# A streaming-encoder step on one core: the edges of the expert stage, and the walk of one eviction

## Chip, core and metric

The kernel runs on one core of a Trainium2 chip. The metric is the device time of one launch in microseconds; lower is better. Several runs of the same kernel give a median, and one more execution is taken with the hardware profiler. Engines are named as in the profile: PE is the tensor engine, DVE the vector engine, ACT the scalar engine, POOL the GpSimd engine and SP the sync engine, which here only issues DMAs.

## What is computed

One layer of a transformer-like encoder for 640 tokens (512 of a prompt, 8 x 16 of samples), D = 1024. The change lies in its last part, a retrieval over 128 x 128 = 16384 single-neuron experts:

```python
s1 = q1 @ sub_keys_1.T ; s2 = q2 @ sub_keys_2.T       # 8 heads, 128 keys each
idx, top_s = top-16 of (top-16 of s1) + (top-16 of s2)  # per token and head
gate = softmax(top_s)
f = sum over the 128 chosen experts of  gelu(x . u[idx]) * gate * v[idx]
y = x + gt2 * rmsnorm(f, g_ffn_post)
```

`u` and `v` are tables of 16384 x 1024 floats, 64 MB each.

## The kernel before

The kernel is a row of phases with a barrier of all engines between them. The last two are the gates stage (`phase_gates`) and the expert stage (`phase_experts`).

The 640 tokens are treated in two ways. The first 256 (`GT` = 2 tiles of 128) are *gathered*: POOL issues 512 indirect DMAs (`rows`), each fetching one expert's row of `u` or `v` for 128 tokens, and DVE works on each row (a dot product, or `vacc += egate * row`). The other 384 (`DN`) are *dense*: every expert is computed for them on PE, and a table of gates, mostly zeros, decides what counts.

**The gates stage** writes that table, `gates[block, key, key, token]`, for 6 blocks of 64 tokens. A *group* is 4 tokens, so there are 96 groups. For each, DVE marks one-hot rows of the keys (`first`, `second`, L1858 to L1863), ACT multiplies three of the four by their gates (`weigh`, L1899), PE multiplies them into a 128 x 128 square per token (L1879), and ACT copies the four squares from PSUM into a staging buffer `stage[e]`, [128, 128 keys, 64 tokens] (the *eviction*, L1906). In ACT's program the weighing of group n+1 stands ahead of the eviction of group n. `stage` has two buffers of 32 KB per partition; SP stores each full one as one DMA of 4 MB (L1843). SP also loads the first four tiles of `u` here.

**The expert stage** goes through 128 chunks (`q`) of 128 experts. For each chunk PE transposes the `u` tile (two halves, L2096), ACT and DVE split it into a high and a low part (`uT_h`, `uT_l`), PE multiplies with the dense tokens ("hidden", 24 matmuls, L2107), ACT takes Gelu (`gl`, L2067), POOL multiplies by the gates of this chunk (`gt`, L2035, the *weighing by gates*), ACT and DVE split that (`a_h`, `a_l`), and PE multiplies it with the split `v` tile ("outputs", 18 matmuls, L2119). PE runs hidden of chunk q, then outputs of chunk q-1. Each engine's order is written out by hand: POOL issues the gathers that are due before each weighing by gates; DVE works on four gathered rows per chunk; SP loads `u`, `vraw` (two buffers) and, for every four chunks, `gt` (two buffers) out of the stored table.

At the end (`finish`, five tiles of 128 tokens, in order) ACT squares the tile with a sum (L2079) and takes the root (L2082), DVE scales and adds `x` (L2183, L2187), and SP stores the tile (L2006).

The places that the change touches: `vraw` of the expert stage lay in the memory of `stage[0]`, as did `v`, `a`, `gl`; `gt` and five of the 12 `rows` buffers lay in `stage[1]`. So SP issued the first `gt` load, and behind it `vraw`, after all table stores had landed (L1981 to L1987).

Of the kernel before, what the change touches and what calls it, by code (L numbers as in the profile page):

```python
# [26 lines left out]
ALU = mybir.AluOpType  # L27
# [1762 lines left out]
TB = 64  # L1790


def phase_gates(nc, A, env):
# [11 lines left out]
    env["env"].update(h=h, u=u)  # L1805
# [29 lines left out]
    with nc.Block() as block:  # L1835
        @block.sync
        def _(sp):
            for i in range(len(u)):
                sp.dma_start(u[i][:], A["u_experts"][0, i * P:(i + 1) * P, :]).then_inc(u_in, 16)
            with sp.Fori(0, BLOCKS // 2) as pair:  # L1840
                for e in range(2):
                    sp.wait_ge(S["table_ready"], pair * (2 * PB) + (e + 1) * PB + G)
                    sp.dma_start(A["gates"][pair * 2 + e], stage[e][:]).then_inc(stored[e], 16)  # L1843
            sp.wait_ge(u_in, 16 * len(u))

        @block.gpsimd
# [38 lines left out]
        def _(act):  # L1885
# [16 lines left out]
            def body(n, g, e, at, token, last):  # L1902
# [3 lines left out]
                act.activation(stage[e][:, :, bass.ds(at, G)].rearrange("p i n -> p n i"), PS[:, g, :].rearrange("p (n i) -> p n i", n=G),  # L1906
# [6 lines left out]
def phase_experts(nc, A, env):  # L1913
# [3 lines left out]
    eidx, egate, htok = (env[k] for k in ("eidx", "egate", "htok"))  # L1917
# [9 lines left out]
    v = [[sb(f"v_{'hl'[s]}{i}", 146 + 8 * i + 4 * s, [P, D], F32R) for s in (HI, LO)] for i in range(2)]  # L1927
    a = [[sb(f"a_{'hl'[s]}{i}", 162 + 3 * i + 1.5 * s, [P, DN], F32R) for s in (HI, LO)] for i in range(2)]
    gl = [sb(f"gl{i}", 168 + 1.5 * i, [P, DN]) for i in range(2)]
    gt = [sb(f"gt{i}", 171 + 6 * i, [P, BLK, QUAD, TB]) for i in range(2)]  # L1930
    EARLY = (10, 62, 66, 70, 74, 78, 203)
# [4 lines left out]
    junk = sb("ej", 114, [P, D])  # L1936
# [4 lines left out]
    v_in, g_in = ([sem(f"ex_{n}_in{i}") for i in range(2)] for n in "vg")  # L1941
    row_in = [sem(f"ex_row_in{i}") for i in range(R)]
    y_out = [sem(f"ex_y_out{i}") for i in range(2)]
    y_dram = [A["y_p"][0, t * P:(t + 1) * P, :] for t in range(PT)] + [A["y_s"].rearrange("b q d -> (b q) d")]

    SLOTS = GT * H * TOPK
    LAG = 2 * TOPK
    steps = [("u", k) for k in range(LAG)]
    for k in range(SLOTS):
        steps.append(("v", k))  # L1950
        if k + LAG < SLOTS:
            steps.append(("u", k + LAG))
# [17 lines left out]
    with nc.Block() as block:  # L1970
        @block.sync
        def _(sp):
            def body(i, first, last):
                for q in range(QUAD):
# [9 lines left out]
                    if not (first and q < 2):  # L1984

                        sp.wait_ge(S["v_lo"], i * QUAD + q - 1)
                    sp.dma_start(vraw[q % 2][:], A["v_experts"][0, bass.ds(i * (QUAD * P) + q * P, P), :]).then_inc(v_in[q % 2], 16)  # L1987

            def gates(i, e, first):

                if not first:

                    sp.wait_ge(S["weighed"], i * QUAD)
# [10 lines left out]
            for t in range(NT):  # L2004
                sp.wait_ge(S["y_ready"], t + 1)
                sp.dma_start(y_dram[t], y[t % 2][:]).then_inc(y_out[t % 2], 16)  # L2006
            sp.wait_ge(y_out[0], 16 * 3)
            sp.wait_ge(y_out[1], 16 * 2)

        @block.gpsimd  # L2010
        def _(pool):
            def gather(n):
                kind, k = steps[n]
# [7 lines left out]
                t, j = divmod(k, H * TOPK)  # L2021
                pool.indirect_dma_start(out=rows[n % R][:], out_offset=None, in_=A["u_experts" if kind == "u" else "v_experts"][0],  # L2022
                                        in_offset=bass.IndirectOffsetOnAxis(ap=eidx[:, t, j:j + 1], axis=0)).then_inc(row_in[n % R], 16)

            for n in range(R - PER):
                gather(n)
            for q in range(NCH):
                for n in range(PER * q + R - PER, min(PER * (q + 1) + R - PER, len(steps))):
                    gather(n)
# [8 lines left out]
        def _(act):  # L2038
# [11 lines left out]

            turned(0, 0)
            turned(0, 1)
            for q in range(NCH):
                if q + 1 < NCH:
# [17 lines left out]
            for t in range(NT):  # L2072
                if t < GT:
                    act.wait_ge(S["summed"], (t + 1) * H * TOPK)
                else:
                    act.wait_ge(S["f_psum"], NCH)
                if t:
                    act.wait_ge(S["f_sq"], t)
                act.activation(junk[:].rearrange("p (b n) -> p b n", b=2), result(t), ACT.Square, accum_out=stat[:, 0, t:t + 1]  # L2079
                               ).then_inc(S["f_sq"], 1)  # L2080
# [159 lines left out]
```

## Time and profile before

| | |
|---|---|
| median of 3 runs (range) | 2402.19 us (2400.85 to 2405.74) |
| profiled execution, its own time | 2401.34 us |
| its span | 2399.6 us |
| PE busy | 2093.4 us, 87% of the span |
| DVE busy | 1635.9 us, 68% |
| ACT busy | 839.6 us, 35% |
| POOL busy | 876.6 us, 37% |
| gates stage | about 995 to 1170 us of the span |
| expert stage | about 1171 us to the end |

Busy time is summed over the whole span, and each stage has its own limit, so the prediction reads the two stages apart. Times of rows are microseconds from the start of the span.

### The profile page before, as it was taken

The page shows a single profiled execution, that of the slowest core. Times are in us where ns is not written, and L with a number is a line of the kernel's source. Part 1 is how long each engine was busy: PE and PEld are TensorE (multiplying, and loading weights), DVE is VectorE, ACT ScalarE, POOL GpSimd, SP SyncE. Part 2 cuts the span into 40 slices and gives each one's busy share as a digit, 9 for nine tenths or more (in the row PEclk, how much of TensorE's full clock was granted, in tenths as well). Part 3 has the DMA queues.
Part 4 walks back from the last instruction along what each step waited for, and adds up shares of the span by engine and source line. Part 5 has one row for each costly group of instructions (what it writes and reads, how often), then busy time and mean ns, then how long its engine had stood idle before and what let it go on. Part 6 is the DMA issues. An engine that isn't in the chain of part 4 may idle for free.

```text
span 2399.6 us, 34976 instructions
## 1 busy us (share of the span) xinstructions
PE 2093.4 (87%) x12419; PEld 1826.7 (76%) x12419; DVE 1635.9 (68%) x3217; ACT 839.6 (35%) x1532; POOL 876.6 (37%) x708
## 2 busy tenths in 40 slices
PE   6997888688897993266499999999999999999997
PEld 6894676466755993155489989899889899999986
DVE  2413355334333899988478888888888888888888
ACT  2303344222321111299533333333333333333333
POOL 0001111000000000100167667767667667777762
PEclk9998999899998996599899999999999999999999
DMA  7311232333221000033699999999999999999994
GB/s 247 107 36 52 88 106 89 119 101 130 104 106 73 1 2 1 35 140 140 262 330 366 366 350 373 361 356 368 347 368 363 357 370 356 367 369 354 368 358 176
DMA packets 193494, 537.67 MB, mean 224 GB/s; under 512 B 19797, under 2 KB 76410, under 8 KB 191610
## 3 DMA queue, kind: packets, MB, share of 16 engines
q1 hardware_dynamic: 119376, 267.53, 31.4%
q0 software_dynamic: 73728, 268.47, 29.3%
q8 instruction: 44, 0.72, 0.1%
q10 hardware_dynamic: 298, 0.55, 0.1%
q14 instruction: 48, 0.39, 0.0%
HBM read 505.35 MB, written 31.15 MB: 224 GB/s over the span
## 4 chain that ended last, share of the span: by engine, by line
PE 47%; DMA 4%; issue 3%; DVE 2%; ACT 2%; SPq 0%; ACTq 0%; DVEq 0%; POOLq 0%; POOL 0%
PE PS L2107 20%; PE PS L2119 19%; PE PS L2096 4%; DMA u<-in_u_experts 3%; PE PS L1879 3%; ACT first L1899 1%; DMA vraw<-in_v_experts 1%; DMA gates<-stage 1%; DVE vacc L2170 0%; DVE first L1862 0%; DVE v_l L2197 0%; DVE rows L2156 0%; DVE yo L2183 0%; DVE yo L2187 0%; ACT stage L1906 0%
## 5 line engine op out<-in xcount | busy, mean ns | idle before, releaser
L2022 POOL DMA_INDIRECT rows<-in_u_experts,eidx x256 | 424.4, 1658 | 247.7 <-POOLq L160 166.9
L2107 PE MATMUL PS<-h_hi,uT_h 128*128 128x384 f32 x1024 | 355.4, 347 | 0.0
L2107 PE MATMUL PS<-h_hi,uT_l 128*128 128x384 f32 x1024 | 345.0, 337 | 0.0
L2107 PE MATMUL PS<-h_lo,uT_h 128*128 128x384 f32 x1024 | 344.0, 336 | 0.0
L2170 DVE SCALAR_TENSOR_TENSOR vacc<-rows,egate,vacc 128x1024 f32<-128x1024 f32 x254 | 329.6, 1298 | 2.2
L2146 DVE TENSOR_TENSOR uT_l<-PS,uT_h 128x512 fp32r<-128x512 f32 x256 | 177.2, 692 | 202.7 <-ACT uT_h L2042 202.7
L2156 DVE SCALAR_TENSOR_TENSOR rows<-rows,htok 128x1024 f32<-128x1024 f32 x256 | 310.1, 1216 | 6.6 <-DMA rows<-in_u_experts,eidx 6.5
L2119 PE MATMUL PS<-v_h,a_h 128*128 128x512 f32 x768 | 310.9, 405 | 0.0
L2119 PE MATMUL PS<-v_l,a_h 128*128 128x512 f32 x768 | 300.0, 391 | 0.0
L2022 POOL DMA_INDIRECT rows<-in_v_experts,eidx x256 | 271.4, 1060 | 58.9 <-issue 43.0
L2042 ACT ACTIVATE uT_h<-PS 128x512 fp32r<-128x512 f32 x256 | 153.1, 598 | 367.4 <-PE PS L2096 367.4
L2119 PE MATMUL PS<-v_h,a_l 128*128 128x512 f32 x768 | 238.1, 391 | 0.0
L2035 POOL TENSOR_TENSOR gl<-gl,gt 128x384 f32<-128x384 f32 x128 | 133.9, 1046 | 236.0 <-ACT gl L2067 236.0
L2107 PEld LDWEIGHTS PS<-h_lo,uT_h 128*128 128x128 f32 x1024 | 194.0, 189 | 0.0
L2107 PEld LDWEIGHTS PS<-h_hi,uT_h 128*128 128x128 f32 x1024 | 193.9, 189 | 0.0
L2107 PEld LDWEIGHTS PS<-h_hi,uT_l 128*128 128x128 f32 x1024 | 193.3, 189 | 0.0
L2096 PE MATMUL PS<-const,u 128*128 128x128 f32 x1024 | 155.9, 275 | 33.0 <-DVE uT_l L2146 25.1
L2067 ACT ACTIVATE gl<-PS 128x384 f32<-128x384 f32 x128 | 62.9, 491 | 335.0 <-PE PS L2107 335.0
L2096 PEld LDWEIGHTS PS<-const,u 128*128 128x128 f32 x1024 | 126.8, 141 | 59.0 <-DVE uT_l L2146 26.0
L2119 PEld LDWEIGHTS PS<-v_h,a_l 128*128 128x128 f32 x768 | 144.3, 188 | 31.3
L1879 PE MATMUL PS<-first,second 128*128 128x128 f32 x768 | 109.7, 287 | 64.8 <-issue 43.4
L2197 DVE TENSOR_TENSOR v_l<-vraw,v_h 128x1024 fp32r<-128x1024 f32 x128 | 156.1, 1220 | 14.7 <-ACT v_h L2062 14.7
(342 smaller groups left out, 3618.1 us busy)
## 6 DMA issues: line engine op xcount, KB each, us to landing
u<-in_u_experts SPq DMA_DIRECT2D x128, 512.0 KB, 8.1
vraw<-in_v_experts SPq DMA_DIRECT2D x128, 512.0 KB, 5.7
gates<-stage SPq DMA_DIRECT2D x6, 4096.0 KB, 11.5
gt<-gates SPq DMA_DIRECT2D x32, 768.0 KB, 9.6
wada_b<-in_w_ada SPq DMA_DIRECT2D x16, 1024.0 KB, 5.1
wada<-in_w_ada SPq DMA_DIRECT2D x8, 1024.0 KB, 11.9
kc<-in_cache_sb_k SPq DMA_DIRECT2D x8, 1024.0 KB, 7.3
vc<-in_cache_sb_v SPq DMA_DIRECT2D x8, 1024.0 KB, 5.4
```

The costliest lines, as they stand in the source:

```text
L1879: mm = pe.matmul(PS[:, g, j * NKEYS:(j + 1) * NKEYS], second[g][:, j, :], first[g][:, j, :], start=True, stop=True)
L2022: pool.indirect_dma_start(out=rows[n % R][:], out_offset=None, in_=A["u_experts" if kind == "u" else "v_experts"][0], in_offset=bass.Indir ...
L2035: pool.tensor_tensor(act_by_block, act_by_block, gt[e][:, :, c, :], ALU.mult).then_inc(S["weighed"], 1)
L2042: act.activation(uT[q % 2][HI][:, 4 * b:4 * b + 4, :], PS[:, 0, :].rearrange("p (k n) -> p k n", k=4), ACT.Copy).then_inc(S["uT_hi"], 1)
L2067: act.activation(gl[q % 2][:], PS[:, 1, 0:DN], ACT.Gelu).then_inc(S["gelu"], 1)
L2096: mm = pe.transpose(PS[:, 0, j * P:(j + 1) * P], u[q % UR][:, k * P:(k + 1) * P], ident)
L2107: mm = pe.matmul(PS[:, 1, 0:DN], uT[q % 2][w][:, k, :], h[m][:, k, :], start=k == 0 and (w, m) == PASSES[0], stop=k == KD - 1 and (w, m) = ...
L2119: mm = pe.matmul(PS[:, 2 + 2 * t + b, :], a[q % 2][w][:, t * P:(t + 1) * P], v[q % 2][m][:, b * 512:(b + 1) * 512], start=fresh and (w, m) ...
L2146: dve.tensor_tensor(uT[q % 2][LO][:, 4 * b:4 * b + 4, :], PS[:, 0, :].rearrange("p (k n) -> p k n", k=4), uT[q % 2][HI][:, 4 * b:4 * b + 4 ...
L2156: dve.scalar_tensor_tensor(out=row[:], in0=row[:], scalar=1.0, in1=htok[:, t, :], op0=ALU.mult, op1=ALU.mult, accum_out=dots[:, t, j:j + 1 ...
L2170: dve.scalar_tensor_tensor(out=vacc[:, t, :], in0=row[:], scalar=egate[:, t, j:j + 1], in1=vacc[:, t, :], op0=ALU.mult, op1=ALU.add).then_ ...
L2197: dve.tensor_tensor(v[q % 2][LO][:], vraw[q % 2][:], v[q % 2][HI][:], ALU.subtract).then_inc(S["v_lo"], 1)
```

## The change

1. The eviction of the gates stage reads PSUM and writes `stage` in another order: keys outside, the group's four tokens inside. Before it was tokens outside, keys inside.
2. The memory map of the expert stage is drawn anew. `vraw` and three `rows` buffers lie where `hT` lay, which is free after POOL has split it (`h_split`). SP loads the first two `vraw` tiles, and POOL issues the first three gathers, in the gates stage behind `h_split`. `rows` has 11 buffers instead of 12.
3. The last of the six table stores is issued as four DMAs of 1 MB (32 keys each). The first `gt` load waits for the first of the four; the second `gt` load, and POOL's gather number 5, wait for all four.
4. The first of the five final tiles, whose rows are all summed after chunk 71, is squared in chunk 72 and finished in chunk 73. Results are written into `vacc` or into one buffer per tile, so no store has to land before the next tile.

The diff, cut to its core:

```diff
+PARTS = 4
+LAG = 2 * TOPK
+AHEAD = 3
...
 def phase_gates(nc, A, env):
...
+    vraw = [sb(f"vraw{i}", 46 + 4 * i, [P, D]) for i in range(2)]
+    rows = [sb(f"rows{i}", at, [P, D]) for i, at in enumerate((54, 58, 62, 10, 203, 176, 180, 184, 188, 192, 196))]
...
-            with sp.Fori(0, BLOCKS // 2) as pair:
-                for e in range(2):
-                    sp.wait_ge(S["table_ready"], pair * (2 * PB) + (e + 1) * PB + G)
-                    sp.dma_start(A["gates"][pair * 2 + e], stage[e][:]).then_inc(stored[e], 16)
+            sp.wait_ge(h_split, 2)
+            for i in range(2):
+                sp.dma_start(vraw[i][:], A["v_experts"][0, i * P:(i + 1) * P, :]).then_inc(v_in[i], 16)
+            for b in range(BLOCKS - 1):
+                sp.wait_ge(S["table_ready"], (b + 1) * PB + G)
+                sp.dma_start(A["gates"][b], stage[b % 2][:]).then_inc(stored[b % 2], 16)
+            sp.wait_ge(S["table_ready"], BLOCKS * PB + G)
+            for i in range(PARTS):
+                keys = slice(i * NKEYS // PARTS, (i + 1) * NKEYS // PARTS)
+                sp.dma_start(A["gates"][BLOCKS - 1, :, keys, :], stage[1][:, keys, :]).then_inc(parts[i], 16)
...
+            pool.wait_ge(h_split, 2)
+            for n in range(AHEAD):
+                gather(pool, A, eidx, steps, rows, row_in, n)
...
-                act.activation(stage[e][:, :, bass.ds(at, G)].rearrange("p i n -> p n i"), PS[:, g, :].rearrange("p (n i) -> p n i", n=G),
+                act.activation(stage[e][:, :, bass.ds(at, G)], PS[:, g, :].rearrange("p (n i) -> p i n", n=G),
                                ACT.Copy).then_inc(S["table_ready"], 1)
...
 def phase_experts(nc, A, env):
...
-    uT = [[sb(f"uT_{'hl'[s]}{i}", 46 + 8 * i + 4 * s, [P, KD, P], F32R) for s in (HI, LO)] for i in range(2)]
+    uT = [[sb(f"uT_{'hl'[s]}{i}", 138 + 8 * i + 4 * s, [P, KD, P], F32R) for s in (HI, LO)] for i in range(2)]
-    vraw = [sb(f"vraw{i}", 138 + 4 * i, [P, D]) for i in range(2)]
-    rows = [sb(f"rows{i}", at, [P, D]) for i, at in enumerate(EARLY + (183, 187, 191, 195, 199))]
+    LATE = 5
-    y = [sb(f"yo{i}", 106 + 4 * i, [P, D]) for i in range(2)]
+    y = [vacc[:, t, :] for t in range(GT)] + [sb(f"yo{i}", 106 + 4 * i, [P, D])[:] for i in range(DT)]
+    first_done = steps.index(("v", H * TOPK - 1)) // PER + 1
...
-                        for stored in env["gates_stored"]:
-                            sp.wait_ge(stored, 16 * (BLK // 2 + 1))
+                        sp.wait_ge(env["gates_stored"][0], 16 * (BLK // 2 + 1))
+                        sp.wait_ge(env["gates_stored"][1], 16 * (BLK // 2))
+                        sp.wait_ge(env["gates_parts"][0], 16)
                         sp.dma_start(gt[0][:], A["gates"][0:BLK, :, 0:QUAD, :].rearrange("b p c n -> p b c n")).then_inc(g_in[0], 16)
...
-                if n == len(EARLY):
-                    for stored in env["gates_stored"]:
-                        pool.wait_ge(stored, 16 * (BLK // 2 + 1))
+                if n == LATE:
+                    for part in env["gates_parts"]:
+                        pool.wait_ge(part, 16)
...
+            act.wait_ge(env["gates_stored"][0], 16 * (BLK // 2 + 1))
             turned(0, 0)
             turned(0, 1)
             for q in range(NCH):
+                if q == first_done:
+                    squared(0)
+                if q == first_done + 1:
+                    rooted(0)
...
+                if q == first_done:
+                    variance(0)
+                if q == first_done + 1:
+                    finish(0)
-            for t in range(NT):
+            for t in range(1, NT):
+                variance(t)
                 finish(t)
```

Three places show how the instructions stand. First SP, from the last stores of the gates stage to its first waits on chunks; before the change the stores are in a loop over pairs of blocks.

```order
L1843 DMA gates<-stage_7322 128x8192
L1842 REGISTER_ALU
L1843 ISA
L1843 DMA gates<-stage_7323 128x8192
L1840 REGISTER_ALU
L1840 COMPARE_AND_BRANCH
L1835 UNCONDITIONAL_BRANCH
L1971 UNCONDITIONAL_BRANCH
L1983 DMA gt_8847<-gates 128x6x256
L1987 DMA vraw_8835<-in_v_experts 128x1024
```

The same place on SP after the change.

```order
L1869 DMA u_7337<-in_u_experts 128x1024
L1872 DMA vraw_7338<-in_v_experts 128x1024
L1872 DMA vraw_7339<-in_v_experts 128x1024
L1875 DMA gates<-stage_7322 128x8192
...
L1879 DMA gates<-stage_7323 128x2048 x4
L1865 UNCONDITIONAL_BRANCH
L2001 UNCONDITIONAL_BRANCH
L2014 DMA gt_8845<-gates 128x6x256
L2019 DMA vraw_7338<-in_v_experts 128x1024
```

The loads of the first two `vraw` tiles have moved from behind the first `gt` load to ahead of all stores, and the last store is four.

Second POOL, from its split of `hT` in the gates stage to its first weighing by gates, before the change: behind the branches twelve gathers stand ahead of that weighing (the first and the last are shown).

```order
L1850 TENSOR_TENSOR h_lo<-hT,h_hi 128x3072
L1835 UNCONDITIONAL_BRANCH
L159 ISA
L2010 UNCONDITIONAL_BRANCH
L2022 DMA rows_8849<-in_u_experts,eidx 128x1024
...
L2022 DMA rows_8860<-in_u_experts,eidx 128x1024
L2035 TENSOR_TENSOR gl_8845<-gl_8845,gt_8847 128x384
```

The same place on POOL after the change.

```order
L1886 TENSOR_TENSOR h_lo<-hT,h_hi 128x3072
L1812 DMA rows_7340<-in_u_experts,eidx 128x1024
L1812 DMA rows_7341<-in_u_experts,eidx 128x1024
L1812 DMA rows_7342<-in_u_experts,eidx 128x1024
L1865 UNCONDITIONAL_BRANCH
...
L1812 DMA rows_7344<-in_u_experts,eidx 128x1024
L1812 DMA rows_7345<-in_u_experts,eidx 128x1024
...
L1812 DMA rows_7350<-in_u_experts,eidx 128x1024
L2065 TENSOR_TENSOR gl_8847<-gl_8847,gt_8845 128x384
```

Three gathers now stand in the gates stage; of the eight that are left ahead of the weighing, the third (`rows_7345`) is the one that waits for all four parts, so six are issued behind that wait.

Third ACT, in chunks 72 and 73 after the change (`htok` takes the Square's unused output, `stat` its sums; a chunk's own rows are `uT_h`, `v_h`, `gl`, `a_h` and now and then `dots`).

```order
L2120 ACTIVATE a_h_8851<-gl_8848 128x384
L2088 ACTIVATE htok,stat<-vacc 128x1024
L2072 ACTIVATE uT_h_8838<-PS 128x512
L2079 ACTIVATE dots<-dots 128x16
...
L2120 ACTIVATE a_h_8849<-gl_8847 128x384
L2093 ACT_TABLE_LOAD
L2093 ACTIVATE stat<-stat 128x1
L2072 ACTIVATE uT_h_8836<-PS 128x512
L2111 ACTIVATE v_h_8843<-vraw_7339 128x1024
L2116 ACT_TABLE_LOAD
L2116 ACTIVATE gl_8848<-PS 128x384
```

The Square, the root and the two table loads are new in the loop; before, these chunks held the other rows alone.

## Rows read from the trace of the kernel before

**Rows 1.** Windows view: stretch, length, busy us (count) by engine, clock, DMA share, GB/s.

```profile
1090.00:1117.00 27.00, 17.97 (x129) 15.38 (x129) 22.65 (x50) 27.00 (x65) 0.00 (x0) 1.00 0.36 155
...
1184.00:1200.00 16.00, 0.00 (x0) 0.00 (x0) 2.47 (x4) 0.00 (x0) 4.68 (x5) 0.57 1.03 403
...
2100.00:2200.00 100.00, 99.95 (x545) 90.79 (x544) 84.00 (x111) 33.43 (x55) 71.51 (x55) 1.00 0.99 366
```

**Rows 2.** Chain that ended last, between the stages: start us, us, what.

```profile
1169.80 14.16 DMA gates<-stage
1184.48 16.41 DMA vraw<-in_v_experts
...
1212.70 4.11 PE PS L2119 x18
```

**Rows 3.** Groups of the gates stage, the eviction: count, busy, mean ns, idle before.

```profile
L1906 ACT ACTIVATE stage<-PS 128x512 f32 (+1 forms) x96 | 118.1, 1230 | 0.9 <-PE PS L1879 0.9
```

**Rows 4.** Timeline, gates stage: its start, then two groups in the middle.

```profile
1010.56 0.96 ACT L1899 ACTIVATE first<-first,sel 128x128 f32<-128x128 f32 x3
...
1100.97 1.28 ACT L1906 ACTIVATE stage<-PS 128x512 f32 x1
...
1101.80 1.19 ACT L1899 ACTIVATE first<-first,sel 128x128 f32<-128x128 f32 x3
...
1103.09 1.13 PE L1879 MATMUL PS<-first,second 128*128 128x128 f32 x8 [0.57 <-issue]
...
1104.35 1.28 ACT L1906 ACTIVATE stage<-PS 128x512 f32 x1
```

**Rows 5.** Timeline, ACT in an early chunk of the expert stage.

```profile
1217.28 0.60 ACT L2042 ACTIVATE uT_h<-PS 128x512 fp32r<-128x512 f32 x1 [2.83 <-PE PS L2096]
1217.78 1.05 ACT L2062 ACTIVATE v_h<-vraw 128x1024 fp32r<-128x1024 f32 x1
```

**Rows 6.** Timeline: SP's four loads, the last eviction, PE's restarts.

```profile
995.40 1.75 SPq L1839 DMA_DIRECT2D u<-in_u_experts  x4
...
1168.60 1.02 ACT L1906 ACTIVATE stage<-PS 128x512 f32<-128x512 f32 x1 [0.33 <-PE PS L1879]
...
1171.21 0.63 PE L2096 MATMUL PS<-const,u 128*128 128x128 f32 x4 [2.64 <-PEq L160]
...
1205.03 1.12 PE L2096 MATMUL PS<-const,u 128*128 128x128 f32 x4 [22.26 <-DVE uT_l L2146]
```

**Rows 7.** Timeline, POOL and ACT at the first weighing by gates.

```profile
1185.96 0.94 POOL L2022 DMA_INDIRECT rows<-in_u_experts,eidx  x1 [0.30 <-issue]
...
1203.85 0.99 POOL L2035 TENSOR_TENSOR gl<-gl,gt 128x384 f32<-128x384 f32 x1 [13.23 <-ACT gl L2067]
...
1204.87 0.52 ACT L2071 ACTIVATE a_h<-gl 128x384 fp32r<-128x384 f32 x1 [0.62 <-POOL gl L2035]
```

**Rows 8.** Tile view of `gt`, over all its 32 loads.

```profile
DMA to landing us min/median/max: 7.9/9.6/14.3
```

**Rows 9.** Timeline, ACT and DVE in a chunk in the middle of the expert stage.

```profile
1717.23 0.60 ACT L2042 ACTIVATE uT_h<-PS 128x512 fp32r<-128x512 f32 x1 [2.84 <-PE PS L2096]
...
1717.86 0.69 DVE L2146 TENSOR_TENSOR uT_l<-PS,uT_h 128x512 fp32r<-128x512 f32 x1 [1.01 <-ACT uT_h L2042]
...
1721.43 0.49 ACT L2067 ACTIVATE gl<-PS 128x384 f32<-128x384 f32 x1 [2.55 <-PE PS L2107]
```

**Rows 10.** Timeline, the last tiles' finish.

```profile
2378.97 1.28 ACT L2082 ACT_TABLE_LOAD   x1
...
2383.04 0.61 PE L2119 MATMUL PS<-v_h,a_l 128*128 128x512 f32 x2
...
2383.77 1.28 DVE L2183 SCALAR_TENSOR_TENSOR yo<-vacc,stat,gffn 128x1024 f32<-128x1024 f32 x1
2384.61 0.20 ACT L2079 ACTIVATION_READ_ACCUMULATOR ej<-PS 128x1 f32 x1
2385.09 1.22 DVE L2187 TENSOR_TENSOR yo<-yo,x 128x1024 f32<-128x1024 f32 x1
2386.24 0.14 DVE L2176 TENSOR_SCALAR stat<-stat 128x1 f32<-128x1 f32 x1
```

More of the change, by code:

```diff
@@ L1790, with gather_order, gather @@
 TB = 64
+PARTS = 4
+SLOTS = GT * H * TOPK
+LAG = 2 * TOPK
+AHEAD = 3
+def gather_order():
+    steps = [("u", k) for k in range(LAG)]
+    for k in range(SLOTS):
+        steps.append(("v", k))
+        if k + LAG < SLOTS:
+            steps.append(("u", k + LAG))
+    return steps
+def gather(pool, A, eidx, steps, rows, row_in, n):
+    kind, k = steps[n]
+    t, j = divmod(k, H * TOPK)
+    slot = n % len(rows)
+    pool.indirect_dma_start(out=rows[slot][:], out_offset=None, in_=A["u_experts" if kind == "u" else "v_experts"][0],
+                            in_offset=bass.IndirectOffsetOnAxis(ap=eidx[:, t, j:j + 1], axis=0)).then_inc(row_in[slot], 16)
 def phase_gates(nc, A, env):
@@ L1804, in phase_gates @@
     u = [sb(f"u{i}", 106 + 4 * i, [P, D]) for i in range(4)]
-    env["env"].update(h=h, u=u)
+    vraw = [sb(f"vraw{i}", 46 + 4 * i, [P, D]) for i in range(2)]
+    rows = [sb(f"rows{i}", at, [P, D]) for i, at in enumerate((54, 58, 62, 10, 203, 176, 180, 184, 188, 192, 196))]
+    v_in = [nc.alloc_semaphore(f"v_in{i}") for i in range(2)]
+    row_in = [nc.alloc_semaphore(f"row_in{i}") for i in range(len(rows))]
+    parts = [nc.alloc_semaphore(f"gates_part{i}") for i in range(PARTS)]
+    steps = gather_order()
+    eidx = env["eidx"]
+    env["env"].update(h=h, u=u, vraw=vraw, rows=rows, v_in=v_in, row_in=row_in, steps=steps, gates_parts=parts)
     h_split, u_in = sem("gt_h_split"), sem("gt_u_in")
@@ L1916, in phase_experts @@
     x, h, u, gffn, stat = (env[k] for k in ("x", "h", "u", "gffn", "stat"))
-    eidx, egate, htok = (env[k] for k in ("eidx", "egate", "htok"))
+    eidx, egate, htok, vraw, rows, v_in, row_in, steps = (env[k] for k in ("eidx", "egate", "htok", "vraw", "rows", "v_in", "row_in", "steps"))
     NCH = NEXP // P
@@ L1979, in body @@
                     if first and q == 0:
-                        for stored in env["gates_stored"]:
-                            sp.wait_ge(stored, 16 * (BLK // 2 + 1))
+                        sp.wait_ge(env["gates_stored"][0], 16 * (BLK // 2 + 1))
+                        sp.wait_ge(env["gates_stored"][1], 16 * (BLK // 2))
+                        sp.wait_ge(env["gates_parts"][0], 16)
                         sp.dma_start(gt[0][:], A["gates"][0:BLK, :, 0:QUAD, :].rearrange("b p c n -> p b c n")).then_inc(g_in[0], 16)
-                    if not (first and q < 2):
-                        sp.wait_ge(S["v_lo"], i * QUAD + q - 1)
+                    if first and q < 2:
+                        continue
+                    sp.wait_ge(S["v_lo"], i * QUAD + q - 1)
                     sp.dma_start(vraw[q % 2][:], A["v_experts"][0, bass.ds(i * (QUAD * P) + q * P, P), :]).then_inc(v_in[q % 2], 16)
             def gates(i, e, first):
-                if not first:
+                if first:
+                    for part in env["gates_parts"][1:]:
+                        sp.wait_ge(part, 16)
+                else:
                     sp.wait_ge(S["weighed"], i * QUAD)
@@ L2020, in gather @@
                     pool.wait_ge(S["dotted" if was == "u" else "summed"], w + 1)
[L2021 to L2026, printed above, removed]
+                gather(pool, A, eidx, steps, rows, row_in, n)
+            for n in range(AHEAD, R - PER):
+                fetch(n)
             for q in range(NCH):
                 for n in range(PER * q + R - PER, min(PER * (q + 1) + R - PER, len(steps))):
-                    gather(n)
+                    fetch(n)
                 e, c = divmod(q % (2 * QUAD), QUAD)
@@ L2049, in activated, with squared, rooted @@
                 act.activation(cols, cols, ACT.Gelu).then_inc(S["dot_gelu"], 1)
+            def squared(t):
+                if t < GT:
+                    act.wait_ge(S["summed"], (t + 1) * H * TOPK)
+                else:
+                    act.wait_ge(S["f_psum"], NCH)
+                if t:
+                    act.wait_ge(S["f_sq"], t)
+                act.activation(junk.rearrange("p (b n) -> p b n", b=2), result(t), ACT.Square, accum_out=stat[:, 0, t:t + 1]
+                               ).then_inc(S["f_sq"], 1)
+            def rooted(t):
+                act.wait_ge(S["f_var"], t + 1)
+                act.activation(stat[:, 0, t:t + 1], stat[:, 0, t:t + 1], ACT.Sqrt).then_inc(S["f_sqrt"], 1)
+            act.wait_ge(env["gates_stored"][0], 16 * (BLK // 2 + 1))
             turned(0, 0)
@@ L2203, in _ @@
                 dve.tensor_tensor(a[q % 2][LO][:], gl[q % 2][:], a[q % 2][HI][:], ALU.subtract).then_inc(S["a_lo"], 1)
-            for t in range(NT):
+                if q == first_done:
+                    variance(0)
+                if q == first_done + 1:
+                    finish(0)
+            for t in range(1, NT):
+                variance(t)
                 finish(t)
```

52 lines of the change are left out of this document (16 added, 36 removed).

## The prediction

> **What bounds the kernel now.** I read the stages apart, with the table of windows first. In the gates stage ACT is busy all the time, 27.00 of 27 us, while PE has 17.97 and DVE 22.65, and the DMAs 0.36 of their time. In the middle of the expert stage PE has 99.95 of 100 us; the DMA share is 0.99, so little room is left there, but PE sets the pace. Between the two lies a stretch of 16 us in which PE does nothing and the DMAs run full [rows 1].
>
> The chain of waits says what that stretch is: the last table store holds 14.16 us from 1169.80 on, then the load of `vraw` another 16.41 us, and the first outputs on PE start at 1212.70 [rows 2]. SP issues `gt` and `vraw` only when the stores have landed; ACT cannot split `v`, and so takes no Gelu and turns no further `u` half; PE, which had done its transposes and the first hidden, waits 22.26 us for `uT_l` [rows 6].
>
> In the gates stage the timeline shows ACT's cadence. An eviction starts at 1100.97, the three weighings behind it at 1101.80, and the eviction two groups on at 1104.35 [rows 4]. So a group takes 3.38 / 2 = 1.69 us, of which the eviction holds ACT 0.83 and the weighings 0.86. There are 96 groups [rows 3], 162 us in all.
>
> **The walk of the eviction.** The same count of elements written in one run, `uT_h` from PSUM, lets the next instruction start after 0.50 us (1217.28 to 1217.78) [rows 5]; the eviction with its steps of 256 bytes needs 0.83. The new order writes runs of four tokens (16 bytes), which should end the write's surcharge, but it reads PSUM in steps of 512 bytes, and no instruction of this trace reads PSUM in such steps. So the price of an eviction is bounded from below by 0.50 (the steps cost nothing on the read side). On the read side the nearest row is the stepped write itself: 0.83 if a stepped read costs what the stepped write does, and 1.16 if its surcharge is double.
> The Trainium skill (SBUF — State Buffer, section "Specifications (TRN2)") has lines of 16 bytes in SBUF and wants at least two hits on each for full speed; by that the new write is free and the old one was not, and the trace's 0.83 against 0.50 agrees. The Trainium skill (PSUM — Partial Sum Buffer, section "Specifications (TRN2)") has lines of only 8 bytes in PSUM and says that patterns which are not contiguous slow matmuls; it does not speak of ACT's reads, and no run so far shows them, but carried over to them it is against this edit, and the 26 us below would be 0.
> I take 0.50, since the two sides are separate streams and only the one on the write side has been seen to be slow.
>
> With 0.50 ACT would need 0.50 + 0.86 = 1.36 us a group. Two other limits come next. The chain through PE: eviction 0.50, then the weighings of the group after next, 0.96 when nothing queues ahead of them, 0.10 until PE starts (1102.99 to 1103.09), PE 1.13, 0.13 until its eviction (1104.22 to 1104.35) [rows 4]: 2.82 for two groups, 1.41 each. And DVE's busy time, 22.65 us for 27 / 1.69 = 16 groups, 1.42 each [rows 1]. I take 1.42: 96 x 0.27 = **26 us less**. With 0.83 it is 0; with 1.16 it is 96 x 0.33 = 32 us more. If the weighings stay as long as they are now (1.19), the chain gives 1.52 and the gain is 16; if ACT's 1.36 holds it is 32.
>
> The three early gathers run on POOL beside DVE's first marks, 0.30 + 0.94 = 1.24 us each [rows 7]: 0 if DVE is not held, 3.7 if it is; I take 1 more.
>
> **The start of the expert stage.** In the times of the old trace: the four parts are the same 4 MB, so the last lands at 1169.80 + 14.16 = 1183.96. Behind it POOL issues six gathers, 6 x 1.24 = 7.4, until 1191.4. The first weighing also needs `gt`. Its load is now issued behind the first part; should the parts share the bandwidth and land together, it is issued at 1184.0 and lands after the median 9.6 [rows 8], at 1193.6. Should it come earlier, POOL is the limit. Then follow the weighing by gates 0.99, `a_h` 0.52 [rows 7], `uT_h` 0.60, `uT_l` 0.69 [rows 9] and PE's transposes 1.12 [rows 6], with four handovers of about 0.1: 4.3 in all, so the first outputs start at 1195.7 (POOL) or 1197.9 (`gt`). I take 1196, as the first part has a head start; against 1212.7 [rows 2] that is **17 us less**.
> PE is ready by then. Three more issues delay the barrier by 3 x 0.44 = 1.3 us (1.75 for four [rows 6]); PE starts at 1172.5 instead of 1171.2, ends the first hidden 11.6 later as now (1205.03 less the wait of 22.26 is 1182.8), and has the second done some 8 us after that, at 1192. So the extra issues cost nothing here; without POOL's wait they would cost 1.3. The bounds: with the slowest `gt`, 14.3 [rows 8], the first outputs start at 1202.6 and the gain is 10; if PE itself is the limit, 1192, it is 21.
> What is late next: the second `gt` and the next `vraw` wait on SP behind `v_lo` of chunk 1, and their DMAs share the bandwidth with POOL's six gathers. They are needed one to three chunks of 9.2 us later. `rows` with 11 buffers issues behind the same row's use as before, since each chunk's four gathers still wait for rows of the chunk before, and loses one row of lead in some ten. I cost this at 0.
>
> **The finish of tile 0 in the middle.** Chunk 72 gets a Square, chunk 73 a root, a table load of 1.28 [rows 10] ahead of it and one ahead of the next Gelu. ACT idles 2.84 us ahead of `uT_h` and 2.55 ahead of `gl` in each chunk [rows 9]; each piece fits one of these. DVE gets the scaling and the addition, 1.28 + 1.22, and small ones, 2.8 us, where it idles 1.01 ahead of `uT_l`. So `uT_l` ends 1.8 late, at 1720.3 in the times of [rows 9]; PE wants it when hidden ends, just before `gl` at 1721.43. Cost 0; without that cover, 2 once.
>
> **The tail.** One tile less, but not one period less. The Squares of the last three tiles need PE's last outputs, which end at 2383.65. The first of them is read out by 2384.81, and DVE takes its sum up only at 2386.24, behind the tile before it [rows 10]. That tile is now done one place earlier, so DVE takes the sum up at 2384.85: **1.4 us less**. The rest follows at the old cadence.
>
> **The sum.** On the profiled execution's 2401.34 (span 2399.6): - 26 + 1 - 17 - 1.4 = 2357.9. The median of the runs is 0.85 above that execution, so **2359 us**.
>
> **Rivals.**
> *The eviction keeps its price.* Reading PSUM in steps costs as much as writing in steps did. For it: that one stepped side costs 0.33 on this engine already. Against it: that was the other memory. Time: 2402.2 - 17.4 (that is 17 + 1.4 - 1) = 2385.
> *The eviction gets dearer, and the kernel slower.* The surcharge doubles, the group takes 0.86 + 1.16 = 2.02 us, 32 more in all; 2402.2 + 32 - 17.4 = 2417. It decides from 17.4 / 96 = 0.18 more per group on, an eviction that holds ACT over 1.01 us. Nothing in the rows shows a step of that price. The Trainium skill's rule on PSUM's lines (same page and section) points to this case or the one before.
> *The stall at the start only moves.* `gt` and the six gathers, now in flight together with the table's last parts, come so late that the first outputs stay near 1212.7. The weighing would have to start at 1208.4, so `gt` to land 24 us behind the parts, where its slowest took 14.3 [rows 8]; the full DMAs of that stretch [rows 1] speak for some delay. With the fast eviction 2402.2 - 26 + 1 - 1.4 = 2376; with the old one no change, 2402.
>
> **How the numbers follow.** Forecast 0.50, same price 0.34, dearer 0.10, stall moved 0.06 (half with each eviction). The forecast's own range, with the ends of its terms, is 2348 to 2378; the first rival's is 2380 to 2394. 2349 to 2391 leaves out the slower case, the unchanged half of the last, and the outer ends of the first two, some 0.2 together. Within 0.2% of the old median (4.8 us, about what these runs can tell) is only that half, 0.03; slower 0.10; faster 0.87.
>
> **What would show it.** Right: evictions of about 0.6 us and starts 1.4 us apart in the gates stage, with DVE or PE and no longer ACT as the one that waits for nobody; no wait of ACT for `vraw`; POOL's first weighing near 24 us behind the last eviction; no gap on PE around chunk 73; four tiles of 3.08 us at the end. Wrong: evictions still 1.2 us or longer (first rivals), a wait of PE for `u` or of DVE for `rows` in the first chunks (third), or one of ACT's table loads ahead of `gl` with PE waiting.

## The result

The changed kernel takes 2369.18 us (median of four runs, 2362.03 to 2375.99); the kernel before, on the same chip, 2403.97. The ratio is 0.9853, 95% interval 0.9816 to 0.989: 35 us less, where 43 were predicted. A second series gave 2367.55 us, 0.9846 (0.9824 to 0.9868). The profiled execution took 2362.03 us, its span 2360.1.

Four marks cut a span into stretches: SP's first `u` load, which opens the gates stage; the end of the last eviction; the start of the first outputs on PE; the end of PE's last matmul. In us, from the timelines of the profiled executions (the experiments' rows are read further down):

| kernel | SP's first `u` load at | gates stage | to the first outputs | outputs to PE's end | tail |
|---|---|---|---|---|---|
| before | 995.4 | 174.2 | 42.8 | 1171.2 | 15.9 |
| changed | 991.9 | 150.4 | 26.3 | 1177.1 | 14.4 |
| changed, again | 1003.1 | 149.6 | 25.7 | 1177.5 | 14.4 |
| e1, walk alone | 995.3 | 149.6 | 43.1 | 1171.2 | 15.9 |
| e2, old walk | 1003.4 | 174.4 | 25.3 | 1178.3 | 14.4 |
| e3, whole store | 1003.6 | 149.6 | 25.1 | 1177.5 | 14.4 |
| e5, `vraw` late | 997.5 | 149.6 | 32.9 | 1167.6 | 14.4 |
| e4, `u` two ahead | 998.3 | 150.4 | 26.4 | 1164.5 | 14.4 |
| e4, again | 996.8 | 149.6 | 25.7 | 1163.0 | 14.4 |
| e6, weighing first | 995.9 | 149.6 | 23.0 | 1171.0 | 14.4 |
| e8, rows by part | 998.6 | 150.3 | 27.6 | 1165.5 | 14.4 |
| e7, POOL weights | 1003.4 | 154.7 | 26.7 | 1180.0 | 14.4 |
| e9, tile 0 at the end | 991.6 | 150.4 | 26.3 | 1180.3 | 15.8 |
| e10, weighing two ahead | 1003.3 | 141.5 | 26.3 | 1164.2 | 14.4 |

So the 39.5 us between the two profiled spans are 3.5 ahead of the gates stage, 23.9 in it, 16.5 at the start of the expert stage, less 5.9 given back in it, and 1.5 at the tail.

**The gates stage.** The eviction's group, then the window that answers to [rows 1], then one group in the timeline:

```profile
L1945 ACT ACTIVATE stage<-PS 128x512 f32 (+1 forms) x96 | 56.6, 589 | 2.3 <-PE PS L1918 2.2
```

```profile
1090.00:1117.00 27.00, 21.30 (x153) 18.23 (x152) 26.20 (x57) 26.97 (x77) 0.00 (x0) 1.00 0.36 156
```

```profile
1100.66 0.58 ACT L1945 ACTIVATE stage<-PS 128x512 f32 x1
...
1101.14 0.98 ACT L1938 ACTIVATE first<-first,sel 128x128 f32<-128x128 f32 x3
1101.39 0.68 DVE L1902 TENSOR_TENSOR second<-const,sel 128x512 f32<-128x512 f32 x1
1102.12 0.60 ACT L1945 ACTIVATE stage<-PS 128x512 f32 x1
...
1102.21 1.13 PE L1918 MATMUL PS<-first,second 128*128 128x128 f32 x8 [0.23 <-DVE second L1902]
...
1103.56 0.57 ACT L1945 ACTIVATE stage<-PS 128x512 f32 x1
```

An eviction takes 589 ns instead of the 1230 of [rows 3]. The 96 of them start between 1004.56 and 1141.68: 137.12 / 95 = 1.443 us a group. ACT and DVE both look full (26.97 and 26.20 of 27). The timeline names DVE as PE's releaser, but the ends say otherwise: `second` ends at 1101.39 + 0.68 = 1102.07, ACT's weighings at 1102.12, and PE starts 0.09 behind these. Nor is DVE's busy time what a group costs it. At the start of the gates stage of the kernel before, with all four buffers of marks free, its `second` starts 1.33 us apart:

```profile
1005.09 0.68 DVE L1863 TENSOR_TENSOR second<-const,sel 128x512 f32<-128x512 f32 x1
...
1006.41 0.68 DVE L1863 TENSOR_TENSOR second<-const,sel 128x512 f32<-128x512 f32 x1
...
1007.74 0.68 DVE L1863 TENSOR_TENSOR second<-const,sel 128x512 f32<-128x512 f32 x1
```

**The start of the expert stage.** The chain of waits from the last eviction on:

```profile
1141.68 0.61 ACT stage L1945
...
1144.11 11.39 DMA gates<-stage
...
1156.29 1.80 POOL rows L1812
...
1164.36 0.93 POOL rows L1812
1165.31 1.02 POOL gl L2065
...
1170.37 1.15 DVE v_l L2238
...
1172.75 14.84 DMA u<-in_u_experts
...
1187.64 0.66 PE PS L2137 x4
```

The first weighing comes 23.0 us behind the end of the last eviction (1142.28), the first outputs at 1168.58. Then something new stands in the chain, a load of `u`. SP's queue says why it is late:

```profile
1157.31 14.56 SPq L2019 DMA_DIRECT2D vraw<-in_v_experts  x2
1171.99 0.38 SPq L2028 DMA_DIRECT2D gt<-gates  x1
1172.75 0.34 SPq L2008 DMA_DIRECT2D u<-in_u_experts  x1
```

The load of `u` for chunk 4 stands behind a `vraw` load that waits for `v_lo` of chunk 1, and behind the second `gt`. It is issued 4.2 us behind the first outputs (1168.58); in the kernel before it was 0.5 (1212.99 against 1212.45, where the timeline has the first outputs). PE's waits in this stretch, and two windows with its granted clock:

```profile
PE PS L2137 <- DVE uT_l L2187: 7.9, 4, 3.6
...
PE PS L2137 <- DMA u<-in_u_experts: 4.0, 1, 4.0
```

```profile
1168.14:1174.20 6.06, 6.06 (x22) 4.98 (x23) 6.06 (x7) 1.67 (x4) 5.27 (x5) 0.72 0.93 329
...
1187.64:1194.05 6.41, 6.41 (x30) 6.37 (x31) 4.12 (x6) 1.54 (x2) 0.34 (x1) 0.73 0.96 380
```

The starts of outputs 0 to 3 are 10.74, 14.92 and 9.18 us apart, where 9.17 is the rule. The 5.75 over in the second are 4.0 of waiting and 1.6 in the hidden behind it (5.75 us instead of 4.17), for the granted clock falls to 1.2 GHz for part of it. The 1.57 over in the first are of the same kind: PE had waited 3.63 us for `uT_l`, and the clock of that window is 0.72. Together 7.3 us, of which the late `u` has 5.75. In the kernel before, PE came out of its wait of 22.26 us just as slowly, but ahead of the first outputs: the transposes at its restart took 1.12 us [rows 6], and the clock from there to 1212.40 is 0.64.

**The middle and the end.** A window around the finish of tile 0 (Square at 1824.55, table loads at 1832.87 and 1837.27), then the variances of the last three tiles:

```profile
1820.00:1860.00 40.00, 40.00 (x220) 36.43 (x219) 36.26 (x49) 17.50 (x28) 27.50 (x21) 1.00 0.98 351
```

```profile
2346.85 0.15 DVE L2217 TENSOR_SCALAR stat<-stat 128x1 f32<-128x1 f32 x1 [0.92 <-ACT htok L2088]
...
2349.93 0.15 DVE L2217 TENSOR_SCALAR stat<-stat 128x1 f32<-128x1 f32 x1
...
2353.01 0.15 DVE L2217 TENSOR_SCALAR stat<-stat 128x1 f32<-128x1 f32 x1
```

PE has no gap, and the tail keeps its period of 3.08 us.

### The profile page after: what moved, and what is told of

Read it like the earlier page. It is cut to its first block, busy times and chain, and to the rows that moved or that the text cites. A ratio compares the mean times of both kernels' runs of the same rounds, so it can differ in the third digit from the quotient of the medians.

```text
span 2360.1 us, 34953 instructions
## 1 busy us (share of the span) xinstructions
PE 2092.5 (89%) x12419; PEld 1826.0 (77%) x12419; DVE 1636.3 (69%) x3217; ACT 817.0 (35%) x1534; POOL 879.9 (37%) x708
## 4 chain that ended last, share of the span: by engine, by line
PE 45%; DVE 6%; DMA 4%; issue 2%; DVEq 1%; SPq 0%; POOL 0%; ACT 0%; POOLq 0%
PE PS L2148 20%; PE PS L2160 20%; PE PS L2137 4%; DMA u<-in_u_experts 4%; DVE second L1902 2%; DVE first L1901 1%; DVE first L1897 1%; DMA gates<-stage 0%; DVE rows L2197 0%; DVE v_l L2238 0%; PE PS L1918 0%; DVE vacc L2211 0%; POOL rows L1812 0%; DVEq L1902 0%; DVE yo L2224 0%
## 5 line engine op out<-in xcount | busy, mean ns | idle before, releaser
L1812 POOL DMA_INDIRECT rows<-in_v_experts,eidx x256 | 424.7, 1659 | 76.8 <-issue 71.2
L1812 POOL DMA_INDIRECT rows<-in_u_experts,eidx x256 | 273.6, 1069 | 207.1 <-POOLq L160 140.7
L2160 PEld LDWEIGHTS PS<-v_h,a_h 128*128 128x128 f32 x768 | 145.0, 189 | 26.4
L2160 PEld LDWEIGHTS PS<-v_l,a_h 128*128 128x128 f32 x768 | 145.2, 189 | 26.0
```

The lines of the kernel that those rows point to most:

```text
L1812: pool.indirect_dma_start(out=rows[slot][:], out_offset=None, in_=A["u_experts" if kind == "u" else "v_experts"][0], in_offset=bass.Indire ...
L2160: mm = pe.matmul(PS[:, 2 + 2 * t + b, :], a[q % 2][w][:, t * P:(t + 1) * P], v[q % 2][m][:, b * 512:(b + 1) * 512], start=fresh and (w, m) ...
```

## The experiments

**The walk, alone and undone.** e1 puts it into the kernel before; e2 takes it out of the changed one.

```diff
-                act.activation(stage[e][:, :, bass.ds(at, G)].rearrange("p i n -> p n i"), PS[:, g, :].rearrange("p (n i) -> p n i", n=G),
+                act.activation(stage[e][:, :, bass.ds(at, G)], PS[:, g, :].rearrange("p (n i) -> p i n", n=G),
```

> The kernel before with the new walk of the eviction alone. Theory: the walk is worth what the gates stage lost between the two traces, 174.2 - 150.4 = 24 us, whatever the rest does; evictions near 0.59 us, groups 1.46 us apart, first outputs still 43 us behind the last eviction: 2403 - 24 = 2379 us. Rival: the phases ahead of the gates stage, which were 3.5 us shorter in the profile after, owe that to the change too: then they stay long here and a later repeat of the change shows them short again. Second rival: a part of the 24 us needs the early loads; then evictions stay over 0.7 us here and the time is over 2385.

> The changed kernel with the old walk of the eviction, all else as changed. Theory: groups 1.69 us apart again; first outputs 26 us behind the last eviction instead of 43 (16.5 less), about 6 us of it given back by waits of PE in the first three chunks, 1.5 less at the tail: 12 less than before, 2391 us. Rival, the prediction's sum, in which nothing is given back: 17 less, 2386 us.

e1: 2376.48 us, ratio 0.9898 (0.9848 to 0.9947); e2: 2394.4 us, 0.9949 (0.9931 to 0.9967). The gates stage is 149.6 to 150.4 us with the new walk and 174.2 to 174.4 without it, whatever surrounds it (the table's rows but e7 and e10, which change the stage itself), and e2's evictions are back at their old length:

```profile
L1945 ACT ACTIVATE stage<-PS 128x512 f32 (+1 forms) x96 | 119.1, 1241 | 0.9 <-PE PS L1918 0.9
```

In e2 the start again gains 17.5 and gives 7.1 back. The 3.5 us ahead of the gates stage are no part of the change: the code there is the same in all kernels, and SP's first `u` load falls between 991.6 and 1003.6 in the fourteen profiles, at 1003.1 in the second one of the changed kernel.

**What the early start rests on.** e3 stores the last table whole; e5 loads the first two `vraw` behind `gt` again.

```diff
-PARTS = 4
+PARTS = 1
```

> The changed kernel with the last table store in one piece. Theory: POOL's six gathers, which wait for the whole table in either case, set the first weighing; gt is then issued about 9 us later, at the landing, and needs 7.9 to 14.4 us where the gathers need 9: the first weighing moves by 0 to 5 us, 2369 to 2374 us. Rival: the head start of the first part is what brings the start forward; then the first weighing and the first outputs come 9 us later, 2378 us.

```diff
-            for i in range(2):
-                sp.dma_start(vraw[i][:], A["v_experts"][0, i * P:(i + 1) * P, :]).then_inc(v_in[i], 16)
...
-                    if first and q < 2:
-                        continue
-
-                    sp.wait_ge(S["v_lo"], i * QUAD + q - 1)
+                    if not (first and q < 2):
+                        sp.wait_ge(S["v_lo"], i * QUAD + q - 1)
```

> The changed kernel with the first two vraw loads back behind the first gt load on SP. Theory: they are now issued behind the first part of the store, near 5 us behind the last eviction, land 8 to 16 us later, so the first Gelu comes no later than 1 or 2 us behind the time at which POOL is done with its gathers: cost 0 to 3 us, 2369 to 2372 us; with the parts it is the release that counts, not the preload. Rival, the chain of the kernel before: vraw's 16.4 us stand in the path again, 10 us or more, 2379 us or more.

e3: 2370.32 us, 0.985 (0.9817 to 0.9884). Beside the preload the four parts bring nothing measurable; the first outputs even come 0.6 to 1.3 us earlier than in the changed kernel's two profiles. With the whole store SP issues `gt` at 1167.13, and POOL weighs right behind its six gathers, so `gt` landed within 7.5 us:

```profile
1173.69 0.94 POOL L1812 DMA_INDIRECT rows<-in_u_experts,eidx  x1 [0.30 <-issue]
1174.66 1.00 POOL L2065 TENSOR_TENSOR gl<-gl,gt 128x384 f32<-128x384 f32 x1
```

e5: 2370.11 us, 0.9856 (0.9825 to 0.9886), no change in the time, but not for my theory's reason. `vraw` stands in the chain again, and the first outputs come 6.6 us later (32.9 instead of 26.3):

```profile
1151.54 16.54 DMA vraw<-in_v_experts
...
1168.10 1.06 ACT v_h L2107
```

Only, PE then does not wait for `u` in the first chunks, and its outputs there are 9.2 us apart: the load of `u` is issued 0.3 us behind the first outputs (1180.20 against 1179.94). The stretch from the first outputs to PE's end is 9.5 us shorter than in the changed kernel, so what the preload brings at the first outputs, the late load of `u` took back, and some 3 us more. The parts count here: `vraw` is issued 4.5 us behind the end of the last eviction, where it was 14.9 in the kernel before, and the first outputs still come 9.9 us earlier than there. The preload with `u` issued in time was not taken out in any run.

**Is `u` late by its place on SP?** e4 issues each later `u` load two places earlier.

```diff
-                    if not first:
+                    if not (first and q < 2) and not (last and q >= 2):
 
-                        sp.wait_ge(S["uT_psum"], i * (2 * QUAD) + 2 * (q + 1 - UR))
-                        sp.dma_start(u[q][:], A["u_experts"][0, bass.ds(i * (QUAD * P) + q * P, P), :]).then_inc(u_in[q], 16)
+                        sp.wait_ge(S["uT_psum"], i * (2 * QUAD) + 2 * (q + 3 - UR))
+                        sp.dma_start(u[(q + 2) % QUAD][:], A["u_experts"][0, bass.ds(i * (QUAD * P) + (q + 2) * P, P), :]).then_inc(u_in[(q + 2) % QUAD], 16)
```

> The changed kernel once more, to set the next three beside it on one chip. Theory: the first outputs 26 us behind the last eviction, then two longer chunks, 10.7 and 14.9 us where 9.17 is the rule, with a wait of PE for u: 2369 us. Rival: the long chunks belong to that one execution, and the waits fall elsewhere in another one; then the first three chunks are 9.2 us apart here.

> The changed kernel with each later u load issued two places earlier on SP, so ahead of vraw loads and of gt loads that it now stands behind. Theory: u is late because of its place in SP's order: the wait of 5.8 us in the third chunk goes, and most of the 7 us of waits for u in later chunks: 6 to 12 us less than the changed kernel, 2357 to 2363 us. Rival: the DMAs are full (0.97 of their time), the wait is one of bandwidth, and u early makes vraw, gt or rows late by as much: within 3 us of the changed kernel.

> The kernel with u two places ahead once more, to stand beside the two others on one chip. Theory: no wait of PE for u, first outputs at +26 us, 2355 us. Rival: its gain over the changed kernel (11 us) was partly the luck of the executions, then it comes near 2362 us.

In the second profile of the changed kernel PE waits 5.0 us for `u` in the same place, and outputs 1 and 2 are 16.2 us apart: that loss does not belong to one execution. The longer first chunk does, it is 9.19 there.

e4: 2356.35 us, 0.9803 (0.9785 to 0.9822), and again 2353.89 us, 0.9793 (0.976 to 0.9825), beside 2367.55 for the changed kernel on the first of these chips. All of PE's waits for `u` in the expert stage are gone; past the barrier one kind is left:

```profile
PE PS L2137 <- DVE uT_l L2187: 7.9, 4, 3.6
```

In the changed kernel the waits for `u` had been 8.5 us in seven places, 4.0 of it the one above. From the first outputs to PE's end it is 12.5 to 14.5 us less. Of the first profile's 12.5, 5.75 are the wait above with the slow clock behind it, and 6.5 are what the later chunks, in which the six other waits lie, took together over their 9.17. The DMAs' full share was no obstacle. In e4 the 1.5 us of slow clock in the first chunk stand (10.72, behind a wait of 3.63 for `uT_l`), in its second profile not (9.19, behind one of 2.39).

**Can the first outputs come earlier still?** e6 and e8 build on e4. e6 weighs first and then issues POOL's late gathers; e8 lets each gather wait only for the parts that its row covers.

```diff
-            for n in range(AHEAD, R - PER):
+            for n in range(AHEAD, LATE):
                 fetch(n)
...
-                for n in range(PER * q + R - PER, min(PER * (q + 1) + R - PER, len(steps))):
-                    fetch(n)
+                if q:
+                    for n in range(PER * q + R - PER, min(PER * (q + 1) + R - PER, len(steps))):
+                        fetch(n)
...
+                if q == 0:
+                    for n in range(LATE, R):
+                        fetch(n)
```

> The kernel with u two places ahead, and on POOL the first weighing put ahead of the gathers that wait for the whole table. Theory: POOL's six gathers (9 us) set the first outputs; without them it is the landing of gt, 8 to 14 us behind its issue: the first outputs 4 to 11 us earlier relative to the last eviction, 4 us or more less than with u ahead alone. Rival: the rows that are fetched later take its place: DVE waits for rows in the second chunk, and what was won is given back, within 2 us of the kernel with u ahead alone.

```diff
-                if n == LATE:
-
-                    for part in env["gates_parts"]:
-                        pool.wait_ge(part, 16)
+                for part in {LATE: (0, 1), LATE + 2: (2,), LATE + 4: (3,)}.get(n, ()):
+                    pool.wait_ge(env["gates_parts"][part], 16)
```

> The kernel with u two places ahead, and POOL's six gathers each waiting only for the parts of the table that lie in its own row. Theory: the parts land one after another, the first 4 us and the last 13 us behind the issue, so POOL is done with its gathers some 4 us earlier, and unlike with the weighing put first no row is late: first outputs at +22.5 to +24 us behind the last eviction instead of +26.3, or at what PE itself allows (second hidden done at +22), and a second chunk without its 1.5 us: 4 to 5 us less than with u ahead alone, 2350 to 2352 us. Rival: gt, issued behind the first part, now shares the DMAs with more rows and lands later than the gathers end; the first weighing stays at +19 or later behind a landing of gt, and the time within 2 us of the kernel with u ahead.

e6: 2355.93 us, 0.9812 (0.9794 to 0.9829); e8: 2359.86 us, 0.9816 (0.9784 to 0.9847): neither beats e4. e6 is level with it on the same chip, as its rival had it; e8 is 6 us slower than e4's second series on the same chip, which is worse than either of its forecasts. In e6 the first outputs come 3 us earlier, and DVE then waits for rows; outputs 0 and 1 are 16.1 us apart:

```profile
DVE rows L2201 <- DMA rows<-in_u_experts,eidx: 2.3, 2, 1.9
```

In e8 the gathers are done early, but `gt` lands late among them, with the DMAs' share at 1.02 from 1152.9 to 1172.8, and the first weighing comes 24.0 us behind the last eviction:

```profile
1152.94 19.82 DMA gt<-gates
```

**What sets the gates stage now?** e7 takes a piece off DVE: it marks four tokens at once, and POOL weights the fourth. e10 builds on e4, and ACT weighs the group after next.

```diff
-                dve.tensor_scalar(first[g][:, G - 1, :], C["iota"], sel[:, 0, col], sel[:, 2, col], ALU.is_equal, ALU.mult)
...
+                pool.wait_ge(S["marked"], n + 1)
+                pool.tensor_tensor(first[g][:, G - 1, :], first[g][:, G - 1, :], sel[:, 2, bass.ds(token + (G - 1), 1)].broadcast_to((P, NKEYS)),
+                                   ALU.mult).then_inc(S["fourth"], 1)
```

> The changed kernel with DVE relieved in the gates stage: it marks all four tokens in one instruction, and POOL weights the fourth, which DVE did with an instruction of its own. Theory: DVE sets the groups of 1.46 us; relieved of about 0.13 us it falls behind the chain through PE (1.41) or ACT (1.36 to 1.46): 5 to 8 us less than the changed kernel, groups of 1.38 to 1.41 us. Rival: ACT, whose pieces fill all its time too, sets them: no change; or POOL's piece is slow (over 0.6 us) and takes the place of the bound: slower.

```diff
-                    weigh(n + 1, (g + 1) % G, token + G)
+                    weigh(n + 2, (g + 2) % G, token + 2 * G)
...
             weigh(0, 0, 0)
+            weigh(1, 1, G)
```

> The kernel with u two places ahead, and in the gates stage ACT weighs the group after next ahead of each eviction instead of the next one, so that PE has its marks a whole group before it needs them. Theory: relieving DVE changed no group, so the 1.44 us are ACT's 0.50 + 0.86 = 1.36 and what an eviction waits for PE, whose matmuls start at the end of the weighing just before; with the weighing a group earlier that wait goes: groups of 1.36 to 1.38 us, 96 x 0.07 = 6 us less than with u ahead alone, near 2348 us. Rival: the groups stay at 1.44 us, because ACT's own dispatch takes the time or because DVE, 1.42 us of work in each, sets them once its marks are wanted a group earlier: 2354 us or, with DVE's start later, more.

e7: 2377.38 us, 0.9888 (0.987 to 0.9906), slower than the changed kernel: of the 10 us on the same chip some 5 lie in the gates stage and 2.5 behind the first outputs, where PE's waits for `u` are longer (12.4 us in 14 places). The groups stay at 1.442 us (evictions from 1020.48 to 1157.46), though DVE's busy time falls to 26.99 of 30 from 29.19 (1060 to 1090 in both); the first eviction comes 17.1 us behind SP's first load instead of 12.6, since POOL's piece queues behind `h_lo` and the gathers. So the theory of DVE falls, though not cleanly: POOL's piece (1101.49 + 0.69) ends with ACT's weighings, and could have set the same pace. e10 decides it: 2350.12 us, 0.9775 (0.975 to 0.9799), with DVE's work as before:

```profile
1100.52 0.82 ACT L1945 ACTIVATE stage<-PS 128x512 f32 x1
1100.54 0.67 DVE L1902 TENSOR_TENSOR second<-const,sel 128x512 f32<-128x512 f32 x1
...
1101.00 1.23 ACT L1938 ACTIVATE first<-first,sel 128x128 f32<-128x128 f32 x3
...
1101.87 0.67 DVE L1902 TENSOR_TENSOR second<-const,sel 128x512 f32<-128x512 f32 x1
1101.88 0.83 ACT L1945 ACTIVATE stage<-PS 128x512 f32 x1
...
1102.32 1.13 PE L1918 MATMUL PS<-first,second 128*128 128x128 f32 x8 [0.23 <-issue]
...
1102.35 1.23 ACT L1938 ACTIVATE first<-first,sel 128x128 f32<-128x128 f32 x3
```

Groups are 1.35 us apart, ACT's own 0.48 + 0.87; the stage loses 8 to 9 us against e4. DVE's share is now full too (30.00 of 30 from 1060 to 1090), but it is ahead: from the 13th to the 73rd group its `second` starts 1.327 us apart (1028.89 to 1108.50), the evictions 1.354 (1032.82 to 1114.06). ACT's pieces look longer (0.82 instead of 0.58) though they start closer together: a piece's length is not what it costs, the next one's start is. e10 has the lowest median of all that were run, but it ran on another chip than e4, and their intervals overlap.

**Tile 0 back at the end.** e9 runs Square, root, variance and scaling of tile 0 with the other tiles.

```diff
-                if q == first_done:
-                    squared(0)
-                if q == first_done + 1:
-                    rooted(0)
...
-            for t in range(1, NT):
+            for t in range(NT):
                 squared(t)
                 rooted(t)
```

> The changed kernel with tile 0 finished at the end again. Theory, the prediction's: one period less at the start of the tail, and nothing in the middle: the stretch from PE's last matmul to the end is 1.4 to 1.5 us longer (15.9 instead of 14.4), and the time 1 to 2 us longer. Rival: the shorter tail comes from the y tiles, which no longer share two buffers; then the stretch stays at 14.4 us. Second rival: the finish in the middle costs PE a gap; then the expert stage is shorter here by 2 us.

2367.96 us, 0.9853 (0.982 to 0.9886). The time can't tell it from the changed kernel; the tail can, 15.8 instead of 14.4. The outputs' stretch is not shorter (1180.3), so the finish in the middle costs nothing that these runs can tell.

## Why the prediction was right

**The walk of the eviction: the mechanism right, the size 2 us off.** 26 us were predicted, 96 x (1.690 - 1.443) = 23.7 measured, 24.6 between e1's gates stage and that of before. The stepped read of PSUM is free: 589 ns beside 599 for `uT_h`, which reads it in one run. The Trainium skill (PSUM — Partial Sum Buffer, section "Specifications (TRN2)") warns of patterns that are not contiguous for matmuls; ACT's read of this case does not show it. What was mis-sized is the group, 1.42, and the engine behind it: I took DVE's busy time for its limit, but DVE does the same work in 1.33 us a group, in e10 and already in the first groups of the kernel before. The chain through PE, which I had at 1.41, sets it: from the eviction at 1100.66 to the one two groups on at 1103.56 its links are 0.48, 0.98, 0.09, 1.13 and 0.22, 2.90 us in all. A sign that I had named did not come: ACT still waits for nobody (26.97 of 27 us). The Trainium skill (Perfetto Trace Analysis, section "Identifying the Most-Contended Engine") goes by the highest occupancy, which is ACT's here; e10 agrees in that ACT sets the pace once PE's wait is gone, but the 0.09 us between 1.44 and 1.35 were a wait that ACT's full share hid.

**Three early gathers: 1 taken, at most 0.8 measured** (150.4 or 149.6 beside e1's 149.6).

**The start of the expert stage: right up to the first outputs.** 17 us were predicted, 16.5 measured; the weighing 23.0 us behind the last eviction, where 24 was said. That the sum came out so close is in part luck, for its terms err both ways: the last part lands 13.2 us behind the last eviction (14.3 in my working), the six gathers take 9.8 us to the weighing (7.4), and from there to the first outputs it is 3.3 (4.3). Of its two limits POOL's gathers stand in the chain. `gt` was some 4 us better: none of the changed kernel's 32 loads took longer than 14.7 us, so the first, issued at 1146.31, had landed by 1161.0, and e6, which waits for it alone, weighs 19.0 us behind the last eviction. Among earlier gathers it takes longer, 19.8 in e8, above the 14.3 that I had as its slowest.

**The step that failed is "What is late next", costed at 0.** I named the second `gt` and the next `vraw`, behind `v_lo` of chunk 1, and asked when they themselves are needed, not what SP issues behind them. That is the load of `u` for chunk 4: 5.75 us in the first profile, 7.1 in the second, slow clock included. Another 1.6 us in the first profile is slow clock behind PE's last wait for `uT_l`, which no term had either; later chunks came out 1.4 shorter, which leaves the 5.9. A wait of PE for `u` had been named as the sign of the third rival; it came true in part, 5.9 of 16.5 us given back, and left the time inside the range.

**The finish in the middle and the tail: right**, 0 and 1.5 us (1.4 predicted); e9 shows that the tail's gain is tile 0's.

The sum: predicted 26 - 1 + 17 + 1.4 = 43.4 less, measured 23.9 + 16.5 - 5.9 + 1.5 = 36.0, and 3.5 of the profiled execution's own.

## What to carry to other kernels

When a stall is removed, follow the queue that carried it: everything that its engine issues in order behind the next wait moves too, and the first item that is late is the new stall, here a load that could have been issued two places earlier at no cost. An engine with a full busy share need not be the bound: compare the ends of all releasers of the one that waits, and try the order of the work before taking work off it. An early load, a divided store or an early release is worth only what the last of the things needed together allows; here the parts were worth nothing beside the preload (e3), and the preload beside the parts only what the late `u` then took back (e5).

## What was not expected of the hardware

- Reading PSUM in steps of 512 bytes costs ACT nothing (589 ns for 128x512 in float32), while writing SBUF in steps of 256 bytes had doubled the instruction (1230 to 1241 ns).
- A wait of PE can cost more than itself: behind the waits of 3.63 and 3.97 us in the changed kernel the clock was granted at 1.2 GHz for a part of what follows (0.72 and 0.73 over some 6 us), and 1.6 us came on top each time. Behind the wait of 2.40 us for `uT_l` in its second profile, and behind one of 3.52 us for `u` in e9, the clock stayed at 1.00.
- `gt`, 768 KB, lands within 7.5 us when it is issued behind the whole store (e3, DMA share 0.86 in that time), and after 19.8 among stores and gathers (e8, 1.02): most of the head start of the first part is lost where the DMAs are full.
- The phases ahead of the gates stage, identical in all kernels, end up to 12 us apart from one execution to the next, more than most of the effects that were looked for here.
